# Output product in three f32r terms, with attention writing the high and low parts of its output

## Chip, cores and metric

One core of one Trainium2 chip. The metric is the device time of one execution in microseconds, from the start of the program to its end. The kernel before takes 3271.62 us (median of 3 runs).

## The reference

One decoder layer on 1024 tokens of width 1024, in float32, followed by a final RMSNorm:

```
h  = x + W_out [ DilatedWindowAttn(heads 0..7) || MLA(heads 8..15) ](RMSNorm(x) @ W_in)
h  = h + PEER(RMSNorm(h))
out = RMSNorm(h)
```

Heads 0 to 7 attend over three dilated windows whose results are merged (written in the kernel as one softmax with a mask of log counts); heads 8 to 15 are dense causal attention on low-rank projections. Each head gives 64 columns, so `mixed` is 1024 x 1024, and the part that the change is about is `h = x + mixed @ w_out`, with w_out 1024 x 1024. PEER then ranks product keys for each token (8 heads, 16 of 16384 experts each) and adds the gated outputs of the experts chosen.

## The kernel before, in words

The program runs stage after stage, with a barrier between: `project_in` (norm, input projection, rotary phases), `attend`, `project_out`, `route` (queries, keys, top 16, and the first expert activations), `spread_gates` and `run_experts`. Tokens are in 8 tiles of 128. Engines are programmed by hand, each with its own instruction list in program order, and meet at semaphores. TensorE is PE in the profile, VectorE DVE, ScalarE ACT, GpSimd POOL, SyncE SP.

`project_in` loads x as four pieces into `res`, which stays in SBUF until the end of `project_out`, where it serves as the residual.

`attend` (L521) works on 8 pairs of heads, four dilated and four dense. A pair p has 8 steps, one for each tile i of queries, and step s = 8p + i handles both heads against (i + 1) tiles of keys. There are 64 steps. Each engine's list is software-pipelined:

- TensorE, step s: `scores(s+1)` (L674), into banks 0 to 3; `turn(s)` (L685), transposes of the probabilities; `weigh(s-1)` (L700), the product with the values, into bank 6 or 7; and, where `due(s)` names any, `turn_head` (L654): transposes of the queries and keys of the next pair, into the same two banks.
- ScalarE, step s: copies of the turned probabilities of head 0 (L750), `exp(s+1)` of both heads (L741), `take(s-1)` (L747), which moves weigh's 128 x 128 result from PSUM to `mixT` in SBUF, and `copy_head` (L734) for the heads that are due.
- VectorE, step s: `masked(s+1, 0)` (L774), a copy of the turned probabilities of head 1 (L724), `masked(s+1, 1)`, further copies, and `normalise(s+1)` of both heads: a reciprocal (L782) and a scaling (L784).

The heads that are due are spread by two lists (L584), relative to the start of the pair before: one piece in each of steps 3, 4, 5, 6 for a dilated pair, pieces in steps 0, 0, 1, 2, 3, 4, 5, 6 for a dense one. What keeps the two output banks from being overwritten is the semaphore `o_out`, raised by `take`:

```
650                    need(pe, o_out, head_steps(p)[n] - 1)     # turn_head in step s: s - 1 counts
696                need(pe, o_out, s - 1)                        # weigh(s)
```

`scores(s)` waits for both `masked(s-1)`; `exp` waits for `masked` and for the `turn` that read the buffer last; `turn(s)` waits for `normalise(s)`.

`project_out` (L805) computes the product by tile: 16 f32 matmuls of 128x512 (L869) into two banks, `add` with the row of `res` (L931), the norm (L901, L905, L943), transposes of the normed row (L878), a copy of it (L948), and its split into `hn_hi` (L910, rounded to f32r) and `hn_lo` (L954, the rest). TensorE works a tile ahead: multiply(1) stands before the transposes of tile 0. SP loads g_ffn, the first w_pq columns and the first keys, and stores each tile's rows as the normed row gets ready.

`route` multiplies in three f32r terms already (L1116: hi x hi, lo x hi, hi x lo, each with 512 columns).

Of the kernel before, what the change touches and what calls it, by code (L numbers as in the profile page):

```python
# [6 lines left out]
P = 128  # L7
# [138 lines left out]
    return v.rearrange("(k p) -> p k", p=P)  # L146


def project_in(core, heads_a, heads_m, mask, mask_in):

    nc, ps, res = core.nc, core.ps, core.res
    I = core.i
    with ExitStack() as ctx:
        sb, sem = core.scope(ctx)
        w_in = sb("w_in", [P, KD, IN_W])
        w_uq = sb("w_uq", [P, 2, UQ_W])
        w_ukv = sb("w_ukv", [P, UKV_W])
        g_mix = sb("g_mix", [P, KD])
# [359 lines left out]
            pair(LAST, False)  # L518


def attend(core, mixT, mask, nat_a, nat_m, w_out, w_out_in):  # L521

    nc, ps = core.nc, core.ps
    PAIRS_A, PAIRS = HA // 2, (HA + HM) // 2
# [3 lines left out]
    with ExitStack() as ctx:  # L528
# [21 lines left out]
        rden_ready, normed, pv_done, o_out = sem("rden_ready"), sem("normed"), sem("pv_done"), sem("o_out")  # L550
# [176 lines left out]
        @block.scalar  # L727
        def _(act):
            def copy_head(p, n):
                k, z, half = pieces(p)[n]  # L730
                w = 2 * dim(p) if in_a(p) else dim(p)
                act.wait_ge(head_turned, pieces_before(p) + n + 1)
                need(act, score_done, 2 * NT * (p - 1))
                nc.scalar.activation(qk[0:w, slot(p, k, z), half * BANK:(half + 1) * BANK], ps[0:w, head_bank(p, n), :],  # L734
                                     ACT.Copy, scale=1.0 if z else -float(dim(p)) ** -0.5).then_inc(head_copied, 1)

            def exp(s, k):
                u, nk = 2 * s + k, (s % NT + 1) * P
                act.wait_ge(masked_ready, u + 1)
                need(act, turned[k], fills_before(s))  # L740
                nc.scalar.activation(pr[:, k, 0:nk], sm[:, k, 0:nk], ACT.Exp, scale=-1.0, bias=least[:, u:u + 1],  # L741
                                     accum_out=den[:, u:u + 1]).then_inc(prob_ready, 1)

            def take(s):
                p, i = s // NT, s % NT
                act.wait_ge(pv_done, s + 1)
                nc.scalar.activation(mixT[:, p, i * P:(i + 1) * P], ps[:, OUT_BANK + s % 2, 0:P], ACT.Copy  # L747
                                     ).then_inc(o_out, 1)

            copy = lambda out, src: nc.scalar.activation(out, src, ACT.Copy)  # L750
            for n in range(len(pieces(0))):
                copy_head(0, n)
            exp(0, 0)
            exp(0, 1)
            for s in range(STEPS):
                for f in range(len(fills(s))):
                    copy_fill(act, copy, s, 0, f)
                if s + 1 < STEPS:
                    exp(s + 1, 0)
                    exp(s + 1, 1)  # L760
                if s:
                    take(s - 1)
                for p, n in due(s):
                    copy_head(p, n)
            take(STEPS - 1)

        @block.vector
        def _(dve):
# [10 lines left out]
            def normalise(s, k):  # L779
# [4 lines left out]
                nc.vector.tensor_scalar(pr[:, k, 0:nk], pr[:, k, 0:nk], rden[:, u:u + 1], None, ALU.mult  # L784
                                        ).then_inc(normed, 1)

            copy = nc.vector.tensor_copy
            masked(0, 0)
            masked(0, 1)
# [14 lines left out]

def project_out(core, mix, w_out, w_out_in, hn_hi, hn_lo, w_raw, keys, pq_in):  # L805

    nc, ps, res = core.nc, core.ps, core.res
    with ExitStack() as ctx:
        sb, sem = core.scope(ctx)
        hn = sb("hn", [P, 2, D])  # L810
# [3 lines left out]
        h_sent = sem("h_sent")  # L814
        full = sb("hnT", [P, 2, KD, P])
        junk = sb("junk_o", [P, D], bf16)
        ss = sb("ss_o", [P, 2])
# [10 lines left out]
        def split_banks(k):  # L828

            return ps[:, 2 + 2 * k:4 + 2 * k, :]  # L830
# [5 lines left out]
            if not (isinstance(n, int) and n == 0):  # L836
                eng.wait_ge(sem_, ONE + n * 2 - 1 + k)

        def row(t, n, k):
            return t[:, n * 2 + k, :]  # L840

        def pairs(pair):
            for n in range(LAST + 1):
# [1 line left out]

        @block.sync
        def _(sp):
            sp.dma_start(g[:, :], core.i["g_ffn"].to_broadcast([P, D])).then_inc(g_in, 16)
            sp.dma_start(w_raw[:, :, :], core.i["w_pq"].rearrange("l (k p) n -> p (l k) n", p=P)[:, :, 0:PQ]
                         ).then_inc(pq_in, 16)  # L850
            sp.dma_start(keys[:, 0, :, :], core.i["sub_keys"].rearrange("l h z n c -> n (l h) z c")[:, 0, :, :]
                         ).then_inc(pq_in, 16)
            for i in range(NT):
                sp.wait_ge(hn_ready, ONE + i + 1)
                if i < GT:
                    sp.dma_start(core.scr_rows[:, i, :], hn[:, i % 2, :]).then_inc(row_sent[i % 2], 16)
                sp.dma_start(core.scr_h[:, i, :], res[:, i, :]).then_inc(h_sent, 16)
            for k in range(2):
                sp.wait_ge(row_sent[k], 16 * len(range(k, GT, 2)))
            sp.wait_ge(h_sent, 16 * NT)  # L860
            sp.wait_ge(pq_in, 32)

        @block.tensor
        def _(pe):
            def multiply(n, k):
                again(pe, h_ready, n, k)
                for c in range(2):
                    for j in range(KD):
                        last = nc.tensor.matmul(split_banks(k)[:, c, :],  # L869
                                                mix[:, j, (n * 2 + k) * P:(n * 2 + k + 1) * P],  # L870
                                                w_out[:, j, c * BANK:(c + 1) * BANK], start=j == 0, stop=j == KD - 1)
                last.then_inc(y_done, 1)

            def turn_hidden(n, k):
# [12 lines left out]
                multiply(n, 1)  # L887
                turn_hidden(n, 0)

            pe.wait_ge(w_out_in, 16)  # L890
            pairs(pair)
            turn_hidden(LAST, 1)

# [1 line left out]
        def _(act):  # L895
            own = Own(act, core.act_own)

            def norms(n, k):
                act.wait_ge(h_ready, ONE + n * 2 + k + 1)
                own.sync()  # L900
                own.mark(nc.scalar.activation(junk[:, :], row(res, n, k), ACT.Square, accum_out=ss[:, k:k + 1]))  # L901
# [11 lines left out]
            def pair(n, first, last):  # L913
# [4 lines left out]
                copy_hi(n, 0)  # L918
                own.restart()

            pairs(pair)
            copy_hi(LAST, 1)

        @block.vector
        def _(dve):
            own = Own(dve, core.dve_own)

            def add(n, k):
                dve.wait_ge(y_done, ONE + n * 2 + k + 1)
                h = row(res, n, k)  # L930
                nc.vector.tensor_tensor(h, split_banks(k).rearrange("p b n -> p (b n)"), h, ALU.add  # L931
                                        ).then_inc(h_ready, 1)

            def normalise(n, k):
# [8 lines left out]
                nc.vector.scalar_tensor_tensor(out=hn[:, k, :], in0=row(res, n, k), scalar=rstd[:, k:k + 1],  # L943
                                               in1=g[:, :], op0=ALU.mult, op1=ALU.mult).then_inc(hn_ready, 1)

            def copy_full(n, k):
# [10 lines left out]
            def pair(n, first, last):  # L957
# [1265 lines left out]
def layer(nc, ins, out):  # L2223
    with ExitStack() as ctx, ExitStack() as outer:
        core = Core(nc, ctx, ins, out)
        with ExitStack() as mid:
            sb, sem = core.scope(mid)
            core.res = sb("res", [P, NT, D])
# [7 lines left out]
            project_in(core, heads["a"], heads["m"], mask, mask_in)  # L2236
            mix = sb("mix_turned", [P, KD, SEQ])
            w_out = sb("w_out", [P, KD, D])
            attend(core, mix, mask, heads["a"], heads["m"], w_out, w_out_in)
            att.close()  # L2240
            hidden = outer.enter_context(ExitStack())
            hn_hi, hn_lo = (hidden.enter_context(nc.sbuf_tensor(n, [P, KD, SEQ], f32r, side="right"))
                            for n in ("hn_hi", "hn_lo"))
# [4 lines left out]
            project_out(core, mix, w_out, w_out_in, hn_hi, hn_lo, w_raw, keys, pq_in)  # L2248
# [63 lines left out]
```

## Time and profile before

| | us |
|---|---|
| median of 3 runs (3264.33 to 3278.61) | 3271.62 |
| the profiled execution | 3271.36 |
| its span | 3269.6 |
| of it `project_in` | 0 to 291 |
| `attend` | 291 to 614 |
| `project_out` | 614 to 742 |
| `route` and all behind it | 742 to 3269.6 |

Over the span TensorE is busy 91% of the time, VectorE 70%, ScalarE 30%, GpSimd 38%; the granted TensorE clock is 0.969 of 2.4 GHz on average. A share of busy time says only which engine a stage leans on; who waits for whom within a step is read from the instructions in order of time. In the rows of the profile, "out<-in" are the tiles written and read, and brackets at the end give the idle time before the instruction and what ended it.

### The profile page before, as it was taken

The numbers are of one execution on the slowest core, as the hardware profiler recorded it, in microseconds if no ns is written. First come the engines' busy times: TensorE is split into PE (matmuls) and PEld (weight loads), VectorE is DVE, ScalarE is ACT, GpSimd is POOL, SyncE is SP. The second block draws the span as 40 slices with busy tenths as digits, with TensorE's granted clock in tenths as the row PEclk, the third lists the DMA queues.
The fourth block names the chain that finished last, engine by engine and source line by source line (L and its number), as shares of the span: only waits on it lengthen the run. The fifth ranks groups of instructions, "written<-read, shape, count | busy, mean of one in ns | idle before, by whom it ended". The sixth has DMA issues, their size and how long they took to land.

```text
span 3269.6 us, 52312 instructions
## 1 busy us (share of the span) xinstructions
PE 2963.8 (91%) x19658; PEld 2423.8 (74%) x19658; DVE 2276.3 (70%) x5468; ACT 987.9 (30%) x1452; POOL 1258.3 (38%) x1088
## 2 busy tenths in 40 slices
PE   7997999997988666689999999999999999999997
PEld 4444666545777656689998888888888888888876
DVE  1213766436999789868977777777777887777435
ACT  2223665212222279722222221122222222222212
POOL 0000000001433400024457767676676776675241
PEclk9998999998999889999999999999999999999998
DMA  5213111112121127798899999999999999999694
GB/s 192 100 56 127 40 47 32 47 48 98 63 69 49 48 59 204 248 297 291 283 356 393 376 377 381 380 383 382 372 383 386 382 391 380 373 387 342 215 326 167
DMA packets 330175, 779.23 MB, mean 238 GB/s; under 512 B 45648, under 2 KB 147280, under 8 KB 328528
## 3 DMA queue, kind: packets, MB, share of 16 engines
q0 software_dynamic: 129024, 469.82, 38.1%
q1 hardware_dynamic: 178512, 288.92, 25.3%
q10 hardware_dynamic: 22400, 17.32, 1.6%
q8 instruction: 148, 2.42, 0.3%
q14 instruction: 91, 0.75, 0.1%
HBM read 699.42 MB, written 72.35 MB: 236 GB/s over the span
## 4 chain that ended last, share of the span: by engine, by line
PE 45%; DVE 11%; DMA 5%; issue 2%; POOL 1%; ACT 0%; SPq 0%; DVEq 0%; ACTq 0%
PE psum L1882 20%; PE psum L1866 19%; PE psum L1908 5%; DVE first L1551 4%; DMA u_ring<-u_rows,eid 3%; DVE one L1544 1%; DMA scr_g<-gates 1%; DVE acc L2071 1%; DVE u_ring L2079 1%; POOL v_ring L1839 1%; DVE u_lo L2035 1%; DVE second L1554 1%; DVE v_lo L2057 1%; DMA v_ring<-v_rows,eidT 1%; DMA v_raw<-v_rows 0%
## 5 line engine op out<-in xcount | busy, mean ns | idle before, releaser
L1839 POOL DMA_INDIRECT v_ring<-v_rows,eidT x448 | 596.1, 1331 | 410.2 <-PE psum L1908 300.6
L1831 POOL DMA_INDIRECT u_ring<-u_rows,eid x448 | 510.8, 1140 | 283.4 <-DVE dots L2079 178.4
L2079 DVE CUSTOM_DVE_ANT_0 u_ring<-u_ring,rows 128x1024 f32<-128x1024 f32 x448 | 544.8, 1218 | 106.6 <-DMA u_ring<-u_rows,eid 105.4
L1866 PE MATMUL psum<-hn_hi_e,u_hi 128*128 128x288 f32 x1792 | 530.1, 296 | 8.4 <-SPq L108 5.0
L1866 PE MATMUL psum<-hn_lo_e,u_hi 128*128 128x288 f32 x1792 | 528.0, 295 | 0.0
L1866 PE MATMUL psum<-hn_hi_e,u_lo 128*128 128x288 f32 x1792 | 527.7, 294 | 0.0
L1882 PE MATMUL psum<-w_hi,v_hi 128*128 128x288 f32 x2048 | 464.0, 309 | 55.1 <-DVE acc L2071 39.9
L2071 DVE TENSOR_TENSOR acc<-psum,acc 128x576 f32<-128x576 f32 x504 | 379.9, 754 | 144.5 <-PE psum L1882 135.8
L1882 PEld LDWEIGHTS psum<-w_hi,v_hi 128*128 128x128 f32 x2048 | 336.6, 194 | 152.8 <-issue 99.3
L1882 PE MATMUL psum<-w_hi,v_lo 128*128 128x288 f32 x2048 | 448.5, 301 | 0.0
L1882 PE MATMUL psum<-w_lo,v_hi 128*128 128x288 f32 x2048 | 448.2, 301 | 0.0
L1866 PEld LDWEIGHTS psum<-hn_hi_e,u_hi 128*128 128x128 f32 x1792 | 337.5, 188 | 14.0 <-issue 14.0
L1882 PEld LDWEIGHTS psum<-w_hi,v_lo 128*128 128x128 f32 x2048 | 339.8, 194 | 0.0
L1882 PEld LDWEIGHTS psum<-w_lo,v_hi 128*128 128x128 f32 x2048 | 339.5, 194 | 0.0
L1866 PEld LDWEIGHTS psum<-hn_lo_e,u_hi 128*128 128x128 f32 x1792 | 336.9, 188 | 0.0
L1866 PEld LDWEIGHTS psum<-hn_hi_e,u_lo 128*128 128x128 f32 x1792 | 336.8, 188 | 0.0
L1969 ACT ACTIVATE psum<-psum 128x576 f32<-128x576 f32 x112 | 71.1, 635 | 854.6 <-PE psum L1866 854.6
L1980 ACT ACTIVATE v_hi<-v_raw 128x1024 fp32r<-128x1024 f32 x128 | 128.8, 1053 | 394.8 <-PE psum L1882 383.0
L2047 DVE TENSOR_TENSOR w<-psum,w 128x576 f32<-128x576 f32 x112 | 84.8, 757 | 206.6 <-ACT psum L1969 206.3
L1908 PE MATMUL psum<-v_ring,strip 128*32 128x512 f32 x1792 | 218.7, 606 | 8.3 <-DMA v_ring<-v_rows,eidT 8.3
L1569 PE MATMUL psum<-second,first 128*128 128x128 f32 x1152 | 147.8, 282 | 72.8 <-DVE second L1554 72.6
L473 PE MATMUL psum<-w_in,hT 128*128 128x512 f32 (+1 forms) x512 | 211.5, 575 | 0.0
(236 smaller groups left out, 4208.4 us busy)
## 6 DMA issues: line engine op xcount, KB each, us to landing
v_raw<-v_rows SPq DMA_DIRECT2D x128, 512.0 KB, 7.2
u_raw<-uT SPq DMA_DIRECT2D x112, 512.0 KB, 8.0
w<-scr_g SPq DMA_DIRECT2D x128, 288.0 KB, 5.9
scr_g<-gates SPq DMA_DIRECT2D x3, 8192.0 KB, 30.6
scr_m<-st_m SPq DMA_DIRECT2D x8, 1024.0 KB, 4.0
w_raw<-in_w_pq SPq DMA_DIRECT2D x8, 1024.0 KB, 7.0
u_raw_r<-uT SPq DMA_DIRECT2D x16, 512.0 KB, 3.6
scr_g<-gates ACTq DMA_DIRECT2D x1, 7680.0 KB, 36.5
```

Of the source, the lines that this page charges most:

```text
L473: last = nc.tensor.matmul(ps[:, 2 + c, 0:width(c)], hT[:, k, j, :], w_in[:, j, c * BANK:c * BANK + width(c)], start=j == 0, stop=j == KD - 1)
L1551: nc.vector.tensor_scalar(first[:, b, t, :], iota_f[:, :], flat[:, 0, at:at + 1], flat[:, 2, at:at + 1], ALU.is_equal, ALU.mult).then_inc( ...
L1569: last = nc.tensor.matmul(slot, first[:, b, t, :], second[:, b, t, :], start=True, stop=True)
L1831: pool.indirect_dma_start(u_ring[:, n % U_RING, :], None, core.i["u_rows"], bass.IndirectOffsetOnAxis(eid[:, x // 2, x % 2, k:k + 1], 0)). ...
L1839: pool.indirect_dma_start(v_ring[:, m % V_RING, :], None, core.i["v_rows"], bass.IndirectOffsetOnAxis(eidT[:, x // 2, col:col + 1], 0)).th ...
L1866: last = nc.tensor.matmul(ps[:, a, 0:COLS], x[:, c, j, :], y[:, j, a * COLS:(a + 1) * COLS], start=m == 0, stop=m == len(terms) - 1)
L1882: last = nc.tensor.matmul(ps[:, OUT_AT + F % OUT_PAIRS * 2 + a, 0:COLS], x[:, c, f * P:(f + 1) * P], y[:, b, c, a * COLS:(a + 1) * COLS], ...
L1908: last = nc.tensor.matmul(ps[k * WIDE:(k + 1) * WIDE, SUM_AT + half, :], strip[:, p % 2, at:at + WIDE], v_ring[:, n % V_RING, half * BANK: ...
L1980: nc.scalar.activation(v_hi[:, c, :], v_raw[:, c, :], ACT.Copy).then_inc(v_hi_ready, 1)
L2047: nc.vector.tensor_tensor(half, ps[:, 0:ACTS, 0:COLS], half, ALU.mult).then_inc(w_ready, 1)
L2071: nc.vector.tensor_tensor(into, ps[:, at:at + 2, 0:COLS], into, ALU.add).then_inc(added, 1)
L2079: nc.vector.tensor_tensor_reduce(out=u, in0=u, in1=rows[:, x % 2, :], scale=1.0, scalar=0.0, op0=ALU.mult, op1=ALU.add, accum_out=dots[:, ...
```

## The change

1. Attention's output is written in two parts, into the places where `hn_hi` and `hn_lo` of the normed rows will lie: `take` on ScalarE writes the f32r-rounded value and raises `hi_out`; a new `low` on VectorE subtracts that from the PSUM value, writes the f32r rest and raises `o_out`. On VectorE `low(s-2)` is the last operation of step s.
2. The output product is 48 f32r matmuls a tile instead of 16 f32 ones. `w_out` is split first, by eight slices: ScalarE rounds into `w_hi`, VectorE subtracts into `w_lo`, which lies where `w_out` lay.
3. `res` is freed after `project_in`; `project_out` loads x again, a tile at a time, into three row buffers from which the rows are also stored.
4. `w_in` moves to the other end of SBUF, with rows of 2048 elements instead of 1952, so that `hn_hi` and `hn_lo` take its place after it.

```diff
@@ attend @@
@@ scalar: take @@
-                nc.scalar.activation(mixT[:, p, i * P:(i + 1) * P], ps[:, OUT_BANK + s % 2, 0:P], ACT.Copy
-                                     ).then_inc(o_out, 1)
+                nc.scalar.activation(mix_hi[:, p, i * P:(i + 1) * P], ps[:, OUT_BANK + s % 2, 0:P], ACT.Copy
+                                     ).then_inc(hi_out, 1)
@@ vector @@
+            def low(s):
+                p, i = s // NT, s % NT
+                dve.wait_ge(hi_out, s + 1)
+                nc.vector.tensor_tensor(mix_lo[:, p, i * P:(i + 1) * P], ps[:, OUT_BANK + s % 2, 0:P],
+                                        mix_hi[:, p, i * P:(i + 1) * P].bitcast(f32), ALU.subtract).then_inc(o_out, 1)
...
                 if s + 1 < STEPS:
                     normalise(s + 1, 0)
                     normalise(s + 1, 1)
+                if s > 1:
+                    low(s - 2)
+            low(STEPS - 2)
+            low(STEPS - 1)
@@ project_out, sync @@
+            x_v = core.i["x"].rearrange("b (i p) d -> p (b i) d", p=P)
+            def load_x(i):
+                sp.dma_start(h[:, i % XB, :], x_v[:, i, :]).then_inc(x_in[i % XB], 16)
+            for i in range(XB):
+                load_x(i)
             sp.dma_start(g[:, :], core.i["g_ffn"].to_broadcast([P, D])).then_inc(g_in, 16)
...
             for i in range(NT):
                 sp.wait_ge(hn_ready, ONE + i + 1)
+                sp.dma_start(core.scr_h[:, i, :], h[:, i % XB, :]).then_inc(h_sent[i % XB], 16)
                 if i < GT:
                     sp.dma_start(core.scr_rows[:, i, :], hn[:, i % 2, :]).then_inc(row_sent[i % 2], 16)
-                sp.dma_start(core.scr_h[:, i, :], res[:, i, :]).then_inc(h_sent, 16)
+                if i + XB < NT:
+                    sp.wait_ge(h_sent[i % XB], 16 * (i // XB + 1))
+                    load_x(i + XB)
@@ tensor: multiply @@
-                for c in range(2):
-                    for j in range(KD):
-                        last = nc.tensor.matmul(split_banks(k)[:, c, :],
-                                                mix[:, j, (n * 2 + k) * P:(n * 2 + k + 1) * P],
-                                                w_out[:, j, c * BANK:(c + 1) * BANK], start=j == 0, stop=j == KD - 1)
+                for j in range(KD):
+                    if n == 0 and k == 0:
+                        pe.wait_ge(w_lo_ready, j + 1)
+                    for t, (x, y) in enumerate(((hn_hi, w_hi), (hn_lo, w_hi), (hn_hi, w_lo))):
+                        for c in range(2):
+                            last = nc.tensor.matmul(split_banks(k)[:, c, :], x[:, j, tokens],
+                                                    y[:, j, c * BANK:(c + 1) * BANK],
+                                                    start=j == 0 and t == 0, stop=j == KD - 1 and t == 2)
@@ scalar, ahead of the tiles @@
+            act.wait_ge(w_out_in, 16)
+            for j in range(KD):
+                nc.scalar.activation(w_hi[:, j, :], w_out[:, j, :], ACT.Copy).then_inc(w_hi_ready, 1)
@@ vector: add, and ahead of the tiles @@
+                dve.wait_ge(x_in[i % XB], 16 * (i // XB + 1))
...
+            for j in range(KD):
+                dve.wait_ge(w_hi_ready, j + 1)
+                nc.vector.tensor_tensor(w_lo[:, j, :], w_out[:, j, :], w_hi[:, j, :].bitcast(f32), ALU.subtract
+                                        ).then_inc(w_lo_ready, 1)
```

`attend` gets `hn_hi` and `hn_lo` for `mixT`; `turn_head` and `weigh` keep their waits for `o_out` word for word.

## Rows read from the trace of the kernel before

**Rows 1.** Busy time by stretch: attention (first two) and the output product.

```profile
core 0: us, PE busy (x) PEld busy (x) DVE busy (x) ACT busy (x) POOL busy (x), PEclk, DMA share, GB/s
291.00:408.00 117.00, 105.77 (x856) 69.49 (x858) 86.40 (x243) 71.60 (x181) 3.51 (x1) 0.93 0.24 78
408.00:614.40 206.40, 188.32 (x1452) 127.17 (x1448) 138.32 (x366) 114.84 (x286) 3.51 (x1) 1.00 0.11 32
614.40:742.00 127.60, 117.95 (x321) 55.80 (x322) 41.14 (x49) 20.01 (x34) 0.00 (x0) 0.97 0.16 63
```

**Rows 2.** Order of time, one dense pair: start us, duration us, engine, line.

```profile
445.50 0.35 DVE L784 TENSOR_SCALAR pr<-pr,rden 128x256 f32<-128x256 f32 x1
...
445.80 0.64 PE L654 MATMUL psum<-ident,qn_m 128*96 128x128 f32 x4
...
449.86 0.64 PE L654 MATMUL psum<-ident,qn_m 128*96 128x128 f32 x4
...
451.46 0.42 DVE L784 TENSOR_SCALAR pr<-pr,rden 128x384 f32<-128x384 f32 x1
...
458.54 0.64 PE L654 MATMUL psum<-ident,qn_m 128*96 128x128 f32 x4
...
460.46 0.55 DVE L784 TENSOR_SCALAR pr<-pr,rden 128x640 f32<-128x640 f32 x1
...
461.78 0.96 DVE L774 CUSTOM_DVE_ANT_0 sm<-psum,mask 128x768 f32<-128x768 f32 x1 [0.77 <-PE psum L674]
...
464.75 0.92 ACT L741 ACTIVATE pr<-sm,least 128x768 f32<-128x768 f32 x1
...
465.12 0.64 PE L654 MATMUL psum<-ident,kn_m 128*96 128x128 f32 x4
...
466.00 0.62 DVE L784 TENSOR_SCALAR pr<-pr,rden 128x768 f32<-128x768 f32 x1
...
479.71 0.64 PE L654 MATMUL psum<-ident,kn_m 128*96 128x128 f32 x4
...
480.80 0.76 DVE L784 TENSOR_SCALAR pr<-pr,rden 128x1024 f32<-128x1024 f32 x1
```

**Rows 3.** Groups of the product's stage, by line.

```profile
L954 DVE TENSOR_TENSOR hn_lo<-hnT,hn_hi 128x1024 fp32r<-128x1024 f32 x8 | 9.8, 1219 | 1.2 <-ACT hn_hi L910 1.2
...
L910 ACT ACTIVATE hn_hi<-hnT 128x1024 fp32r<-128x1024 f32 x8 | 8.3, 1043 | 3.7 <-DVE hnT L948 3.7
```

**Rows 4.** Order of time, the first masked operation of attention.

```profile
295.18 0.29 DVE L774 CUSTOM_DVE_ANT_0 sm<-psum,mask 128x128 f32<-128x128 f32 x1 [11.07 <-PE psum L674]
```

**Rows 5.** Order of time on TensorE, behind idle stretches.

```profile
614.47 27.70 PE L869 MATMUL psum<-w_out,mix_turned 128*128 128x512 f32 x64 [1.78 <-PEq L99]
...
778.94 3.61 PE L1116 MATMUL psum<-hn_hi,w_hi 128*128 128x512 f32 x8 [1.88 <-issue]
...
910.48 2.13 PE L1116 MATMUL psum<-hn_hi,w_hi 128*128 128x512 f32 x8 [3.37 <-DVE w_lo L1409]
...
956.08 3.35 PE L1116 MATMUL psum<-hn_hi,w_hi 128*128 128x512 f32 x8 [3.49 <-DVE w_lo L1409]
...
1093.21 2.29 PE L1096 MATMUL psum<-hn_hi,u_hi_r 128*128 128x288 f32 x8 [2.25 <-ACT u_hi_r L1170]
```

**Rows 6.** Busy time near the start of attention.

```profile
303.00:309.00 6.00, 5.65 (x22) 2.96 (x24) 3.78 (x14) 3.04 (x9) 0.00 (x0) 0.50 1.03 409
```

**Rows 7.** Order of time on TensorE: the same scores in pairs 0 and 1.

```profile
299.37 1.65 PE L674 MATMUL psum<-qk_turned 64*128 64x384 f32 x4 [0.76 <-DVE least L774]
...
313.52 1.56 PE L674 MATMUL psum<-qk_turned 64*128 64x512 f32 x8
...
338.78 0.92 PE L674 MATMUL psum<-qk_turned 64*128 64x384 f32 x4
...
348.45 1.56 PE L674 MATMUL psum<-qk_turned 64*128 64x512 f32 x8
```

**Rows 8.** Order of time on TensorE, f32r matmuls of the routing stage.

```profile
768.32 2.03 PE L1116 MATMUL psum<-hn_hi,w_hi 128*128 128x512 f32 x8
770.19 2.03 PE L1116 MATMUL psum<-hn_lo,w_hi 128*128 128x512 f32 x8
```

**Rows 9.** DMA issue of w_out: KB each, median us from issue to landing.

```profile
w_out<-in_w_out SPq DMA_DIRECT2D x1, 4096.0 KB, 16.0
```

More of the change, by code:

```diff
@@ L146, in column, with project_in @@
     return v.rearrange("(k p) -> p k", p=P)
-def project_in(core, heads_a, heads_m, mask, mask_in):
+def project_in(core, w_in, heads_a, heads_m, mask, mask_in):
     nc, ps, res = core.nc, core.ps, core.res
@@ L154, in project_in @@
         sb, sem = core.scope(ctx)
-        w_in = sb("w_in", [P, KD, IN_W])
         w_uq = sb("w_uq", [P, 2, UQ_W])
@@ L518, in _, with attend @@
             pair(LAST, False)
-def attend(core, mixT, mask, nat_a, nat_m, w_out, w_out_in):
+def attend(core, mix_hi, mix_lo, mask, nat_a, nat_m, w_out, w_out_in):
     nc, ps = core.nc, core.ps
@@ L549, in attend @@
         copied = [sem(f"copied{k}") for k in range(2)]
-        rden_ready, normed, pv_done, o_out = sem("rden_ready"), sem("normed"), sem("pv_done"), sem("o_out")
+        rden_ready, normed, pv_done = sem("rden_ready"), sem("normed"), sem("pv_done")
+        hi_out, o_out = sem("hi_out"), sem("o_out")
         zero_low, zero_high = sem("zero_low"), sem("zero_high")
@@ L802, in _, with project_out @@
                     normalise(s + 1, 1)
-def project_out(core, mix, w_out, w_out_in, hn_hi, hn_lo, w_raw, keys, pq_in):
-    nc, ps, res = core.nc, core.ps, core.res
+                if s > 1:
+                    low(s - 2)
+            low(STEPS - 2)
+            low(STEPS - 1)
+def project_out(core, w_out, w_lo, w_out_in, hn_hi, hn_lo, w_raw, keys, pq_in):
+    nc, ps = core.nc, core.ps
+    XB = 3
     with ExitStack() as ctx:
         sb, sem = core.scope(ctx)
+        w_hi = sb("w_out_hi", [P, KD, D], f32r)
+        h = sb("h", [P, XB, D])
         hn = sb("hn", [P, 2, D])
@@ L813, in project_out @@
         row_sent = [sem(f"row_sent{k}") for k in range(2)]
-        h_sent = sem("h_sent")
+        x_in = [sem(f"x_in_o{k}") for k in range(XB)]
+        h_sent = [sem(f"h_sent{k}") for k in range(XB)]
+        w_hi_ready, w_lo_ready = sem("w_hi_ready_o"), sem("w_lo_ready_o")
         full = sb("hnT", [P, 2, KD, P])
@@ L837, in again, with row @@
                 eng.wait_ge(sem_, ONE + n * 2 - 1 + k)
-        def row(t, n, k):
-            return t[:, n * 2 + k, :]
+        def row(n, k):
+            return h[:, (n * 2 + k) % XB, :]
         def pairs(pair):
@@ L854, in _ @@
                 sp.wait_ge(hn_ready, ONE + i + 1)
+                sp.dma_start(core.scr_h[:, i, :], h[:, i % XB, :]).then_inc(h_sent[i % XB], 16)
                 if i < GT:
                     sp.dma_start(core.scr_rows[:, i, :], hn[:, i % 2, :]).then_inc(row_sent[i % 2], 16)
-                sp.dma_start(core.scr_h[:, i, :], res[:, i, :]).then_inc(h_sent, 16)
+                if i + XB < NT:
+                    sp.wait_ge(h_sent[i % XB], 16 * (i // XB + 1))
+                    load_x(i + XB)
             for k in range(2):
                 sp.wait_ge(row_sent[k], 16 * len(range(k, GT, 2)))
-            sp.wait_ge(h_sent, 16 * NT)
+            for k in range(XB):
+                sp.wait_ge(h_sent[k], 16 * len(range(k, NT, XB)))
             sp.wait_ge(pq_in, 32)
@@ L866, in multiply @@
                 again(pe, h_ready, n, k)
-                for c in range(2):
-                    for j in range(KD):
-                        last = nc.tensor.matmul(split_banks(k)[:, c, :],
-                                                mix[:, j, (n * 2 + k) * P:(n * 2 + k + 1) * P],
-                                                w_out[:, j, c * BANK:(c + 1) * BANK], start=j == 0, stop=j == KD - 1)
+                tokens = slice((n * 2 + k) * P, (n * 2 + k + 1) * P)
+                for j in range(KD):
[6 more added lines that the diff above has]
+                                                    start=j == 0 and t == 0, stop=j == KD - 1 and t == 2)
                 last.then_inc(y_done, 1)
@@ L900, in norms @@
                 own.sync()
-                own.mark(nc.scalar.activation(junk[:, :], row(res, n, k), ACT.Square, accum_out=ss[:, k:k + 1]))
+                own.mark(nc.scalar.activation(junk[:, :], row(n, k), ACT.Square, accum_out=ss[:, k:k + 1]))
                 own.sync()
@@ L929, in add @@
                 dve.wait_ge(y_done, ONE + n * 2 + k + 1)
-                h = row(res, n, k)
-                nc.vector.tensor_tensor(h, split_banks(k).rearrange("p b n -> p (b n)"), h, ALU.add
+                i = n * 2 + k
+                dve.wait_ge(x_in[i % XB], 16 * (i // XB + 1))
+                nc.vector.tensor_tensor(row(n, k), split_banks(k).rearrange("p b n -> p (b n)"), row(n, k), ALU.add
                                         ).then_inc(h_ready, 1)
@@ L942, in normalise @@
                     dve.wait_ge(row_sent[k], 16 * n)
-                nc.vector.scalar_tensor_tensor(out=hn[:, k, :], in0=row(res, n, k), scalar=rstd[:, k:k + 1],
+                nc.vector.scalar_tensor_tensor(out=hn[:, k, :], in0=row(n, k), scalar=rstd[:, k:k + 1],
                                                in1=g[:, :], op0=ALU.mult, op1=ALU.mult).then_inc(hn_ready, 1)
@@ L2225, in layer @@
         core = Core(nc, ctx, ins, out)
+        hidden = outer.enter_context(ExitStack())
+        with nc.sbuf_tensor("hn_hi", [P, KD, SEQ], f32r, side="right") as hn_hi, \
+                nc.sbuf_tensor("hn_lo", [P, KD, SEQ], f32r, side="right") as hn_lo:
+            pass
+        w_in = hidden.enter_context(nc.sbuf_tensor("w_in", [P, KD, 2 * SEQ], f32, side="right"))
         with ExitStack() as mid:
-            sb, sem = core.scope(mid)
-            core.res = sb("res", [P, NT, D])
+            _, sem = core.scope(mid)
             att = ExitStack()
@@ L2235, in layer @@
             clear_counts(nc, (mask_in, w_out_in))
[L2236 to L2239, printed above, removed]
+            with ExitStack() as front:
+                core.res = front.enter_context(nc.sbuf_tensor("res", [P, NT, D], f32))
+                project_in(core, w_in, heads["a"], heads["m"], mask, mask_in)
+            with nc.sbuf_tensor("w_out_lo", [P, KD, D], f32r) as w_lo:
+                pass
+            w_out = mid.enter_context(nc.sbuf_tensor("w_out", [P, KD, D], f32))
+            attend(core, hn_hi, hn_lo, mask, heads["a"], heads["m"], w_out, w_out_in)
             att.close()
-            hidden = outer.enter_context(ExitStack())
-            hn_hi, hn_lo = (hidden.enter_context(nc.sbuf_tensor(n, [P, KD, SEQ], f32r, side="right"))
-                            for n in ("hn_hi", "hn_lo"))
             w_raw = hidden.enter_context(nc.sbuf_tensor("w_raw", [P, KD, PQ], f32, side="right"))
@@ L2247, in layer @@
             clear_counts(nc, (pq_in,))
-            project_out(core, mix, w_out, w_out_in, hn_hi, hn_lo, w_raw, keys, pq_in)
+            project_out(core, w_out, w_lo, w_out_in, hn_hi, hn_lo, w_raw, keys, pq_in)
         with ExitStack() as peer:
```

1 line of the change is left out of this document (removed).

## The prediction

> **What bounds the kernel now.** I read the busy time by stage first. Attention runs from 291 to 614 us, the output product from 614 to 742; TensorE is busy 90, 91 and 92% of the three stretches, at a granted clock of 0.93, 1.00 and 0.97 [rows 1]. So TensorE bounds both stages that the diff touches, and two kinds of edit can move the time: TensorE work taken away, and TensorE made to wait. VectorE has room on average (86.40 + 138.32 us busy in 323) [rows 1], but what counts is when it is done within a step, and for that I read the order of time.
>
> In a step s of attention TensorE issues scores(s+1), turn(s), weigh(s-1) and, in 40 of the 64 steps, turn_head, the transposes that prepare the next pair of heads. Two lists in the code give the 40: steps 3 to 6 of the first three pairs, and steps 0 to 6 of pairs 3 to 6 (two pieces in their step 0): 12 + 28. ScalarE and VectorE meanwhile do exp(s+1) and normalise(s+1), each of two heads. The trace shows TensorE starting turn_head BEFORE the second normalise(s+1) has ended: at 465.12 against 466.62, right behind weigh(s-1), while the second exponential had begun only at 464.75 [rows 2]. Today this is free, since turn_head waits only for the take of step s-2, done by ScalarE a step earlier.
>
> **The change in attention.** ScalarE's take stays, now writing the high part; rounding costs it nothing (a 1024-wide copy into f32r takes 1043 ns, with 128x1024 f32 in) [rows 3]. New is low(s-2) on VectorE, 64 in all, a 128x128 operation with one operand in PSUM; the nearest row of that shape, engine and source is 0.29 us [rows 4]. 64 x 0.29 = 19 us in a stage where VectorE idles some 98 us: as work it is covered. But o_out is now raised by low, and low(s-2) stands in VectorE's order BEHIND both normalise(s+1). turn_head in step s waits for s-1 counts of o_out, that is for low(s-2). So TensorE now waits in each of the 40 steps until VectorE has finished the next step's normalisation, and only then issues turn_head and, behind it, scores(s+2). Before, scores(s+2) covered exactly that latency.
>
> The price of one wait is: end of the second normalise, plus 0.29 for low, minus the start of turn_head today. From the pairs of [rows 2]:
> step 0 of a pair: 445.50+0.35+0.29-445.80 = 0.34;
> step 1: 451.46+0.42+0.29-449.86 = 2.31;
> step 3: 460.46+0.55+0.29-458.54 = 2.76;
> step 4: 466.00+0.62+0.29-465.12 = 1.79;
> step 6: 480.80+0.76+0.29-479.71 = 2.14.
> Steps 2 and 5 read the same way give 2.55 and 1.98. The pattern repeats in all four long blocks (13.9 each) and, as steps 3 to 6, in three short ones (8.6 each): 4 x 13.9 + 3 x 8.6 = 81.4 us. A release from VectorE to TensorE adds about 0.05 each: 2 us.
>
> Does the delay stay, or is it made up? exp(s+2) follows turn(s+1), and masked(s+2) follows scores(s+2): at 461.78 VectorE had been idle 0.77 us for them [rows 2]. Both follow turn_head on TensorE, so a late turn_head moves the whole loop. What is given back are TensorE's present waits for VectorE in these steps, 3 to 4 us by my count. Where no head is due (24 steps) low sits ahead of the next masked and costs at most 0.29 in the few that VectorE bounds: 2 to 3 us; the last low adds 0.35 to the end. These cancel. Attention: **+82 us**, between 70 (more absorbed) and 85. weigh(s-1) waits for low(s-3) too, which follows the normalise that turn(s) needs anyway: nothing. ScalarE's copy_head and SP's loads for the next heads stand behind turn_head and come later with it; they have a step and more of room.
>
> **The clock.** Each wait is a stretch of idle TensorE, 1.8 to 2.8 us long in steps 1 to 6. What the trace shows of such stretches is mixed [rows 5]: after 1.88 us idle eight 512-column matmuls took 3.61 us, after 3.49 us 3.35, but after 3.37 us 2.13; after 2.25 us eight of 288 columns took 2.29. The stretch from 303 to 309 has a granted clock of 0.50 (1.2 GHz) [rows 6]. Of nine idle stretches from 1.5 to 1.8 us, in the routing stage and before the product, none was followed by slow matmuls; of six from 1.8 to 3.9 us five were (the longest of the nine, 1.78, and four of the six have their rows [rows 5]). What the low clock costs: the same steps took 313.52-299.37 = 14.15 us in pair 0, nearly all of it at half clock, and 348.45-338.78 = 9.67 in pair 1 [rows 7]: 4.5 lost in 14.1, 0.32 us per us. If half of the 36 long waits let the clock fall, for 6 us each (about 3 in the routing stage, 12 at the start of attention, where TensorE was busy 5.65 of 6 us and still slow [rows 6]), that is 18 x 6 x 0.32 = **+35 us**. The bounds are 0 and 36 x 8 (about one lengthened step) x 0.32 = 92.
>
> **The change in the product.** Two tiles of 16 f32 matmuls each take 27.70 us, 13.8 a tile [rows 5] (two records per matmul). In their place come 48 f32r matmuls of the same 128x512 shape. The routing stage runs just that: eight from 768.32 to 770.19, 0.234 us each [rows 8], so 48 are 11.2 us. Saved: 2.55 x 8 = 20.4 us, if TensorE stays the bound, and it does: VectorE has five operations near 1.22 us in a tile of 12 and ScalarE less.
> Against it, ahead of the first tile: ScalarE makes w_hi in 8 copies of 1.04, VectorE w_lo in 8 of 1.22 [rows 3]. The first matmul starts after one of each, 2.3 us, and then TensorE's six matmuls per slice (1.4) are slower than VectorE's next slice (1.22), so the rest is hidden. The idle stretch before the product thus grows from 1.78 [rows 5] to about 4.4 us, longer than any that kept the clock; some 4.6 us at half speed do 2.3 us of work, another 2.3 us lost. Sum: -20.4 + 2.3 + 2.3 = **-15.8 us**.
> The residual rows now come by tile: three loads of 512 KB stand on SP's queue ahead of g_ffn, w_raw and keys. By 4096 KB in 16.0 us [rows 9] the first 2 MB land in about 8 us, and the first addition is due after 2.3 + 11.2. Later rows start after the store of the tile three before, 512 KB each way, about 2 us each by the same row, and have two tiles of time: nothing, or at worst one late tile, 5 us. w_raw and keys are needed 110 us later. w_in's rows are wider in SBUF and elsewhere; the same bytes and matmuls: nothing.
>
> **Sum.** The profiled run took 3271.36 us for a span of 3269.6, 0.3 below the median of 3271.62. 3271.4 + 82 + 35 - 16 = **3372 us**.
>
> **The rivals.**
> (a) The wait comes, but the clock holds, in attention and at the product's start: 3271.4 + 82 - 18 = 3336. For it: the clock in 408 to 614 is 1.00 with small gaps everywhere [rows 1]. Against it: five of the six stretches above [rows 5]. 0.22.
> (b) The half clock stays through nearly all of the steps concerned, since TensorE did not leave it for 12 us at the start [rows 6, 7]: 3271.4 + 82 + 92 - 16 = 3429. 0.12. The Trainium skill, TensorE: Matmul & The Clock Gate, section "HAM oscillation — how this bites in real kernels", says that a kernel whose bursts of matmuls alternate with waits can have its clock throttled anew at every burst. By this rule it would come out as (b); the trace agrees in five stretches of the six and not in the one of 3.37 us.
> (c) The other side: the wait is hidden. It decides by one order, low(s-2) against weigh(s-1): if VectorE reached low before TensorE ends weigh, only the product's gain is left, 3271.4 - 16 + 2 = 3257. Weigh would have to last 2 to 3 us longer, or the exponentials start earlier, and they wait for turn(s). 0.05, mostly within 0.5% (16 us, about what a measurement of this kernel can tell from no change).
> (d) The product does not run at the routing stage's rate (the w slices or the row loads pace it), so that the gain is nil, and attention is as forecast: 3388. 0.06.
> Forecast: 0.55.
>
> **Numbers.** The range goes from 3325 (rival a with 10 us more absorbed) to 3425 (short of b); beyond it lie most of b, and c. Faster 0.02, same 0.04, slower 0.94.
>
> **What would show it.** In the trace of after: TensorE's transposes of natural heads (the qn and kn tiles) idle some 80 us in all, released by VectorE's subtraction into the low part, none of it before; their idle is 1.8 to 2.8 each, 0.3 in step 0; attention lasts 400 to 445 us instead of 323, with a granted clock below 1.00 in many stretches; tiles of the product begin 12.1 us apart instead of 14.6. It is wrong if those transposes start right behind weigh, if the clock column stays at 9 in attention while the span grows by more than 90, or if the product's stage is not shorter by 10 to 20 us.

## The result, and the profile after

The changed kernel takes 3359.88 us (median of 4 runs, 3350.44 to 3364.98) against 3270.23 for the kernel before (4 runs, one more than ahead of the prediction): a ratio of 1.0269, 95% interval 1.0236 to 1.0302, 90 us slower. The forecast was 3372, within 3325 to 3425. The profiled execution took 3357.79 us, for a span of 3356.0, 86.4 more than the span before.

The page of the kernel after, its slices of TensorE's busy time and of its granted clock, 84 us each:

```profile
PE   8997776788888856679999999999999999999997
PEclk9997889998999979999999999999999999999998
```

Attention lies in slices 4 to 9. TensorE is down to 6 to 8 tenths there, and the granted clock is at 7, 8 and 8 in slices 4 to 6. By stretches (us, busy time, granted clock, share and rate of the DMA), TensorE in attention from its first instruction to its last:

```profile
core 0: us, PE busy (x), PEclk, DMA share, GB/s
293.75:361.00 67.25, 53.44 (x364) 0.81 0.34 110
361.00:455.00 94.00, 70.76 (x530) 0.87 0.07 18
455.00:506.00 51.00, 39.05 (x273) 0.80 0.11 32
506.00:708.60 202.60, 151.49 (x1142) 1.00 0.09 24
```

Where [rows 1] had 90 and 91% busy, it is now 79, 75, 77 and 75%, and the clock of 0.81 to 0.87 lasts until 506 us. Then it is 1.00, while the busy share stays as low. Who waited for whom in the same stage (us in total, times, the longest):

```profile
PE psum L654 <- issue: 64.9, 33, 2.7
PE psum L654 <- DVE hn_lo L790: 13.0, 7, 2.7
PE psum L654 <- ACT qk_turned L734: 3.1, 4, 0.8
```

TensorE is idle 64.9 + 13.0 = 77.9 us before the transposes of the next heads, 40 times, at most 2.7. Seven of them the trace ascribes to the new subtraction (`low`, L790), 33 to nothing that it shows ("issue"); before the change there was only the third row. That the 33 too are waits for `low` shows in the order of time: in all 40 the transposes start 0.06 or 0.10 us after the end of a `low`. Step 1 of a pair, on VectorE and TensorE:

```profile
511.57 0.42 DVE L784 TENSOR_SCALAR pr<-pr,rden 128x384 f32<-128x384 f32 x1
511.91 0.28 DVE L790 TENSOR_TENSOR hn_lo<-psum,hn_hi 128x128 fp32r<-128x128 f32 x1
```

The second scaling ends at 511.99, `low` at 512.19, and the transposes start at 512.29. One pair of heads in order of time, to be laid beside [rows 2]:

```profile
505.93 0.61 PE L654 MATMUL psum<-ident,qn_m 128*96 128x128 f32 x4 [0.29 <-issue]
...
512.29 0.61 PE L654 MATMUL psum<-ident,qn_m 128*96 128x128 f32 x4 [2.26 <-issue]
...
518.35 0.61 PE L654 MATMUL psum<-ident,kn_m 128*96 128x128 f32 x4 [2.48 <-issue]
...
525.51 0.61 PE L654 MATMUL psum<-ident,qn_m 128*96 128x128 f32 x4 [2.70 <-issue]
...
533.45 0.61 PE L654 MATMUL psum<-ident,kn_m 128*96 128x128 f32 x4 [1.74 <-issue]
...
542.40 0.61 PE L654 MATMUL psum<-ident,qn_m 128*96 128x128 f32 x4 [1.99 <-issue]
...
552.19 0.61 PE L654 MATMUL psum<-ident,kn_m 128*96 128x128 f32 x4 [2.07 <-issue]
...
560.71 0.61 PE L654 MATMUL psum<-ident,qn_m 128*96 128x128 f32 x4 [0.29 <-issue]
```

Each long step has its idle time in brackets: 2.26, 2.48, 2.70, 1.74, 1.99, 2.07, and 0.29 in step 0. From one step 0 to the next it is 560.71 - 505.93 = 54.78 us, at full clock; before, 42.69 (from 445.80 to the next step 0):

```profile
488.49 0.64 PE L654 MATMUL psum<-ident,qn_m 128*96 128x128 f32 x4
```

The last `take` of attention and the product, after:

```profile
708.61 0.28 ACT L747 ACTIVATE hn_hi<-psum 128x128 fp32r<-128x128 f32 x1 [1.47 <-PE psum L700]
...
713.03 1.22 PE L899 MATMUL psum<-w_out_hi,hn_hi 128*128 128x512 f32 x2 [4.47 <-DVE w_out_lo L1005]
...
714.90 1.05 PE L899 MATMUL psum<-w_out_lo,hn_hi 128*128 128x512 f32 x2
...
715.76 1.05 PE L899 MATMUL psum<-w_out_hi,hn_hi 128*128 128x512 f32 x2
...
721.48 0.63 PE L899 MATMUL psum<-w_out_hi,hn_hi 128*128 128x512 f32 x2
...
721.95 0.63 PE L899 MATMUL psum<-w_out_hi,hn_lo 128*128 128x512 f32 x2
...
738.34 1.03 PE L908 MATMUL psum<-ident,hn 128*128 128x128 f32 x8
...
750.46 1.03 PE L908 MATMUL psum<-ident,hn 128*128 128x128 f32 x8
...
823.90 0.69 PE L1141 MATMUL psum<-ident,keys 128*128 128x128 f32 x2 [6.21 <-SPq L1101]
```

The product starts after 4.47 us of idle time instead of 1.78 [rows 5] and at half clock: a pair of matmuls starts 0.86 us behind the one before it at 715.76, and 0.47 at 721.95, which is 0.234 us a matmul. The tiles' transposes come 750.46 - 738.34 = 12.12 us apart instead of 14.61. From the last take to the first transposes of the routing stage (L1141) it is 115.3 us against 129.2 before.

The 86.4 us of the span: `project_in` +2.5 (293.75 against 291.26 for attention's first transposes), attention +93.4 (414.9 against 321.5, first transposes to last take), product -13.9, everything behind it +4.4. The first and the last are not the change's: in the other kernels below, attention starts anywhere from 290.4 to 293.7 us, whether `w_in` lies at the one end or the other, and the stages after the product last 2523 to 2530 us, against 2528 before the change and 2532 here.

### The profile page after: what moved, and what is told of

It reads as the page before. It is cut to its first block, busy times and chain, and to the rows that moved or that the text cites. A ratio compares the mean times of both kernels' runs of the same rounds, so it can differ in the third digit from the quotient of the medians.

```text
span 3356.0 us, 52665 instructions
## 1 busy us (share of the span) xinstructions
PE 2968.6 (88%) x19786; PEld 2461.5 (73%) x19786; DVE 2300.2 (69%) x5540; ACT 999.6 (30%) x1460; POOL 1263.8 (38%) x1088
## 4 chain that ended last, share of the span: by engine, by line
PE 43%; DVE 11%; DMA 5%; issue 3%; POOL 1%; ACT 0%; SPq 0%; DVEq 0%; ACTq 0%
PE psum L1919 19%; PE psum L1903 19%; PE psum L1945 5%; DVE first L1588 4%; DMA u_ring<-u_rows,eid 3%; DVE one L1581 1%; DVE acc L2108 1%; DMA scr_g<-gates 1%; DVE u_ring L2116 1%; POOL v_ring L1876 1%; DVE u_lo L2072 1%; DVE v_lo L2094 1%; DVE second L1591 1%; DMA v_ring<-v_rows,eidT 1%; DMA v_raw<-v_rows 0%
```

## The experiments

Each was timed beside the kernel before on the same chip. Attention's length is taken as above.

**e1_low_early.** The theory is one of order, so the first run changes the order alone:

```diff
-                if s > 1:
-                    low(s - 2)
-            low(STEPS - 2)
+                if s:
+                    low(s - 1)
             low(STEPS - 1)
```

> After, with low(s-1) instead of low(s-2) at the end of VectorE's step s, so that o_out stands a step earlier for turn_head. Theory (turn_head's wait behind the next normalise is the whole loss): the 78 us of idle time before the transposes L654 are gone, the clock in attention is 1.00 from about 312 us on as in before, and only the product's gain of some 10 to 16 us is left: 3250 to 3262. Rival (64 more operations on VectorE, or the f32r parts, cost the time): it stays above 3330. Rival (the wait goes to another place: low(s-1) now waits for take(s-1), and VectorE with it): idle time of VectorE before low of 0.3 us or more in each of 64 steps, and 3270 to 3290.

3254.66 us (3250.24 to 3256.27), ratio 0.9952 (0.9937 to 0.9967): faster than before by 14 us and than the changed kernel by 105. Waits, and the line of `low` in attention:

```profile
PE psum L654 <- ACT qk_turned L734: 3.1, 4, 0.8
L790 DVE TENSOR_TENSOR hn_lo<-psum,hn_hi 128x128 fp32r<-128x128 f32 x63 | 18.0, 285 | 7.5 <-ACT hn_hi L747 7.5
```

The idle time before the transposes is gone but for the 3.1 us that were there before; 64 subtractions are still made. `low` now waits for ScalarE's take, 7.5 us in all where the rival wanted 19, and nobody pays: attention is 320.4 us long, 1 less than before. So neither the work nor the new layout costs anything; the place in VectorE's order does.

**e2_low_between.** A middle dose:

```diff
                 if s + 1 < STEPS:
                     normalise(s + 1, 0)
-                    normalise(s + 1, 1)
                 if s > 1:
                     low(s - 2)
+                if s + 1 < STEPS:
+                    normalise(s + 1, 1)
```

> After, with low(s-2) between the two normalise(s+1) instead of behind both. Theory: each long wait gets shorter by the time from the end of the first to the end of the second scaling (0.9 to 1.1 us by the trace), times 36, so 32 to 40 us less idle before L654, and fewer falls of the clock: 3300 to 3325. Rival (the number of operations or the clock alone counts, not where low stands): within 5 us of after, 3355 to 3365.

3286.45 us (3284.05 to 3294.03), ratio 1.0056 (1.0035 to 1.0077): 14 us below the expected band. The waits, and TensorE in attention from 312 us on:

```profile
PE psum L654 <- issue: 34.1, 30, 1.6
PE psum L654 <- DVE hn_lo L790: 6.8, 6, 1.6
```

```profile
312.00:648.50 336.50, 275.38 (x2240) 1.00 0.11 32
```

The idle time fell by 37 us, to 40.9, as expected, and the longest is 1.6 us. What was not expected: the clock never fell after 312 us. Attention is 354.8 us, 33.4 more than before, so 40.9 us of waits cost 33.4: 7.5 us are made up elsewhere.

**e3_wait_alone.** The kernel before, with nothing but the wait:

```diff
                     need(pe, o_out, head_steps(p)[n] - 1)
+                    pe.wait_ge(normed, 2 * (head_steps(p)[n] + 2))
```

> Before, with one wait more: turn_head waits until both normalise(s+1) are done. No low, no f32r product, res kept. Theory: 36 waits of 1.5 to 2.5 us and 4 of 0.05, 82 - 40 x 0.29 = 70 us, and the clock's share of 15 to 30: 3355 to 3370. Rival (the loss comes from low as work, or from the new layout of SBUF): under 3300.

3359.06 us (3357.86 to 3371.64), ratio 1.0286 (1.0262 to 1.0309): attention's loss with no f32r part at all, 90.4 of the 93.4 us (411.9 against 321.5). That the time is the changed kernel's own is chance: that one has the product's 13.9 us taken off and 6.9 us added outside both stages. Its waits, and two of its transposes:

```profile
PE psum L655 <- DVE pr L785: 63.7, 32, 2.7
PE psum L655 <- ACT mix_turned L748: 11.9, 6, 2.5
```

```profile
517.81 0.78 PE L655 MATMUL psum<-ident,kn_m 128*96 128x128 f32 x4 [1.70 <-DVE pr L785]
...
528.41 1.06 PE L655 MATMUL psum<-ident,qn_m 128*96 128x128 f32 x4 [1.94 <-DVE pr L785]
```

75.6 us idle, 70 expected. At 528.41, after 1.94 us of idle time, four transposes take 1.06 us instead of 0.61: the wait alone brings the clock down as well, here also after 506 us (the mean over the rest of attention):

```profile
506.00:702.30 196.30, 151.50 (x1085) 0.95 0.08 22
```

The expectation took the whole 0.29 us of `low` off each wait, 11.6 in all; the idle time is only 2.3 us under the changed kernel's 77.9. The order of time shows why. Step 1 of a pair here:

```profile
611.77 0.42 DVE L785 TENSOR_SCALAR pr<-pr,rden 128x384 f32<-128x384 f32 x1
612.45 0.61 PE L655 MATMUL psum<-ident,qn_m 128*96 128x128 f32 x4 [2.21 <-DVE pr L785]
```

From the end of the second scaling to the transposes it is 612.45 - 612.19 = 0.26 us, and 512.29 - 511.99 = 0.30 in the changed kernel; over the 40 waits the means are 0.23 and 0.29. So the release by the scaling alone takes nearly as long as `low` with its own release, and 40 x 0.06 = 2.4 us are the difference.

**e4_work_alone.** The kernel before, with the work and no wait:

```diff
+        spare = sb("spare", [P, P], f32r)
...
+            def low(s):
+                p, i = s // NT, s % NT
+                dve.wait_ge(o_out, s + 1)
+                at = mixT[:, p, i * P:(i + 1) * P]
+                nc.vector.tensor_tensor(spare[:, :], at, at, ALU.subtract)
...
                     normalise(s + 1, 1)
+                if s > 1:
+                    low(s - 2)
```

> Before, with 64 subtractions of 128x128 on VectorE at the place of low(s-2), reading mixT and writing a scrap tile, for which nobody waits. Theory: hidden in VectorE's idle time, 0 to 4 us: 3270 to 3274. Rival (VectorE is the bound of attention's steps): +19 us or more, 3289 and above.

3271.57 us (10 runs, 3267.33 to 3279.25), ratio 1.0008 (0.9998 to 1.0018). 62 operations of 284 ns in VectorE's list, for steps 0 to 61, are hidden: attention is 320.4 us long, 1 less than before. They read SBUF, where those of the changed kernel read PSUM, and last as long.

**e5_kept_warm.** The changed kernel, with the wait kept and its idle time filled:

```diff
+                if p and head_steps(p)[n] % NT:
+                    pe.wait_ge(masked_ready, 2 * (head_steps(p)[n] + 2))
+                    for _ in range(FILL):
+                        nc.tensor.matmul(ps[:, 0, 0:P], v_of(p - 1)[:, 0, :], v_of(p - 1)[:, 0, :],
+                                         start=True, stop=True)
                 if p:
                     need(pe, o_out, head_steps(p)[n] - 1)
```

`FILL` is 7. The idle matmuls write bank 0 and so wait for the masks that read it (`masked_ready`).

> After, with seven matmuls of 128x128 f32 (1.5 us in all, by the transposes' rate) that nobody reads, into bank 0, ahead of turn_head's wait in the 36 long steps. The wait itself stays: turn_head starts no earlier. Theory (the clock took about 23 us of attention's 93): granted clock 1.00 in attention from about 312 us on, TensorE's idle before L654 down to some 25 to 30 us, and 3335 to 3345. Rival (the clock costs nothing, since the path runs over the other engines): within 5 us of after, 3355 to 3365. Rival (matmuls in the way delay turn_head): above 3370.

3324.68 us (3322.98 to 3326.04), ratio 1.0168 (1.0153 to 1.0183): 35 us less than the changed kernel for more work, more than the theory gave (26 and 23 less than the two later executions of the changed kernel, below). Order of time on TensorE in one step, the wait that is left, and the stage by stretches:

```profile
461.14 1.83 PE L653 MATMUL psum<-v_more 128*128 128x128 f32 x14
...
463.08 0.64 PE L660 MATMUL psum<-ident,qn_m 128*96 128x128 f32 x4
...
471.48 0.64 PE L660 MATMUL psum<-ident,kn_m 128*96 128x128 f32 x4 [0.16 <-DVE hn_lo L796]
```

```profile
core 0: us, PE busy (x), PEclk, DMA share, GB/s
290.80:312.00 21.20, 17.09 (x90) 0.69 0.79 273
312.00:682.60 370.60, 336.15 (x2720) 1.00 0.09 27
```

The fourteen records at 461.14 are the seven idle matmuls; behind them the transposes wait 0.3 us at most. They still start 0.06 to 0.10 us after the end of `low`, in four of the 40 steps 0.13 to 0.19, so the wait itself is kept. The clock is 1.00 from 312 us to the end. Attention is 391.9 us: 23.0 less than in the changed kernel at the same waits, and 70.4 more than before. That splits attention's 93.4 us: 70.4 for the waits, 23.0 for the clock. The other 12 of the 35 us lie outside attention (3 before it, and the stages behind it, where the two kernels are the same): not explained, and of the size by which those stages differ between executions.

**e6_f32_product.** e1_low_early, with the product as one f32 term of the high part, and no split of w_out:

```diff
...
-                    for t, (x, y) in enumerate(((hn_hi, w_hi), (hn_lo, w_hi), (hn_hi, w_lo))):
-                        for c in range(2):
-                            last = nc.tensor.matmul(split_banks(k)[:, c, :], x[:, j, tokens],
-                                                    y[:, j, c * BANK:(c + 1) * BANK],
-                                                    start=j == 0 and t == 0, stop=j == KD - 1 and t == 2)
+                for c in range(2):
+                    for j in range(KD):
+                        last = nc.tensor.matmul(split_banks(k)[:, c, :], hn_hi[:, j, tokens].bitcast(f32),
+                                                w_out[:, j, c * BANK:(c + 1) * BANK], start=j == 0, stop=j == KD - 1)
...
```

> e1_low_early with the product in one f32 term, 16 matmuls a tile of the high part with w_out, without the split of w_out; left out of the computation: the low part of attention's output. Attention, loads and stores as in e1. Theory: tiles 14.6 us apart instead of 12.1 and a start without the 4.5 us idle: +20 - 5 = +15 against e1's 3254.7, so 3266 to 3273, level with before. Rival (e1's gain comes from attention or from the row loads, not from the product): within 4 us of e1.

3269.77 us (12 runs, 3262.28 to 3276.63), ratio 0.9996 (0.9986 to 1.0007): 15.1 more than e1 by the medians, 14 by the ratios (the two ran on different chips), and level with before. So e1's gain is the three-term product's. In this kernel the stretch from the last take to the routing stage's transposes is 740.84 - 611.57 = 129.3 us, the 129.2 of before, though its residual rows come by tile: the new loads are hidden.

**e7_first_slice.** e1_low_early, with the first slice of w_out split in attention's last two steps (`w_first`, 4 KB a partition):

```diff
@@ attend, scalar, ahead of step 62's copies @@
+                    nc.scalar.activation(w_first[:, j, :], w_out[:, j, :], ACT.Copy).then_inc(first_hi, 1)
@@ attend, vector, behind step 63's copies @@
+                nc.vector.tensor_tensor(w_lo[:, j, :], w_out[:, j, :], w_first[:, j, :].bitcast(f32), ALU.subtract
+                                        ).then_inc(first_lo, 1)
@@ project_out @@
-            for j in range(KD):
+            for j in range(AHEAD, KD):
```

> e1_low_early with the first of the eight slices of w_out split in attention's last two steps, where ScalarE and VectorE wait for TensorE. Theory: the product starts some 1.8 us after attention instead of 4.5, the clock holds there (saves 2.3 to 2.8), then one wait of up to 1 us for the second slice: 4 to 5 us less than e1, 3249 to 3252. Rival (the split delays attention's last steps by as much): no difference from e1.

3252.92 us (3246.31 to 3253.87), ratio 0.9942 (0.9930 to 0.9955) against e1's 0.9952: the intervals overlap, so no difference can be told. The product's start:

```profile
613.80 0.71 PE L917 MATMUL psum<-w_first,hn_hi 128*128 128x512 f32 x2 [2.12 <-PEq L99]
...
616.15 1.22 PE L917 MATMUL psum<-w_out_hi,hn_hi 128*128 128x512 f32 x2 [0.65 <-DVE w_out_lo L1023]
```

The product starts after 2.12 us of idle time, and the first six matmuls run at full speed. Then TensorE waits 0.65 for the second slice, and the matmuls behind it take twice the time: the fall of the clock was not avoided, only moved. The 0.65 us are not its cause, since the clock is down from about 615.2 us on and that wait begins at 615.50. Nor do the 2.12 us decide it by their length: in e6_f32_product the product starts after the same idle time and the clock holds. The clock by stretches in e7:

```profile
613.00:615.20 2.20, 1.40 (x6) 1.00 0.29 37
615.20:619.00 3.80, 3.15 (x9) 0.51 0.95 371
```

The first matmuls and the clock in e6:

```profile
613.64 2.81 PE L895 MATMUL psum<-w_out,hn_hi 128*128 128x512 f32 x6 [2.12 <-PEq L99]
...
613.00:617.00 4.00, 3.36 (x8) 1.00 0.57 176
```

From the last take to the routing stage it is 113.9 us against 115.0 in e1.

**e8_after_again, e9_after_third.** Two more executions of the changed kernel, with their profiles:

> The changed kernel once more, unchanged, for a second profile. In the first one the clock fell in attention only up to about 505 us, though the same waits of 1.7 to 2.7 us went on to 660. If the falls depend on where a wait happens to lie, and not on the step of the program, this profile has them in other stretches, and attention (415 us in the first) is 400 to 430 us long, with idle time before L654 again at 76 to 80 us. Rival (the steps of the second half cannot bring the clock down): it is again 1.00 from 505 us on and attention within 2 us of 415.

> As e8_after_again: a third profile, with the half clock in stretches of its own, or, by the rival, in the same ones as in the first.

3350.39 and 3347.30 us, one run each. TensorE in the second profile, from 361 us on:

```profile
361.00:455.00 94.00, 73.11 (x528) 0.84 0.07 18
455.00:506.00 51.00, 38.76 (x274) 0.80 0.12 33
506.00:707.20 201.20, 150.82 (x1138) 1.00 0.08 24
```

Attention is 415.8 and 414.4 us long, with 78.1 us idle before the transposes in both; the clock is 0.84, 0.80 and 1.00 in these stretches in both. The falls end at the same place, about 500 us, in three executions of three, though the stretches before differ somewhat (0.87 against 0.84 between 361 and 455 us), so chance from one execution to the next does not spread them. Nor is it that the later steps could not bring the clock down: in e3_wait_alone it is 0.95 from 506 us to the end of attention, at waits of the same length. What decides it is open.

## Why the prediction was right

The mechanism came as forecast, and both of its terms were too large: the wait's by 11.6 us and the clock's by 12.0. That the sum is no further off is in part luck, as 6.9 us outside both stages went the other way.

**The wait.** The order in the code was read rightly: `low(s-2)` behind both `normalise(s+1)` holds up `turn_head`, and e1, which moves one line, takes all of it away; e3 brings it back by itself. Its size, step by step, was forecast as 0.34, 2.31, 2.55, 2.76, 1.79, 1.98 and 2.14, and measured 0.29, 2.26, 2.48, 2.70, 1.74, 1.99 and 2.07; 81.4 + 2 in sum against 77.9. The release from VectorE to TensorE that the forecast added at 0.05 is there, 0.06 or 0.10 us. What it left out is that `low` starts 0.08 us before the end of the scaling (511.91 against 511.99), so that from that end to the transposes it is 0.29 us and not 0.29 + 0.05; and that the idle time is counted from the end of the matmuls before, which is later than the start of `turn_head` in the trace of before (449.93 against 449.86 in step 1).

**Whether the delay stays.** Forecast: given back and added cancel, +82 in all, with 70 as the lower bound. Measured: +70.4 (e5). 77.9 us of waits cost 7.5 less than their sum, the same 7.5 as in e2 with half the waits. 3.4 of it are the older waits of `turn` and `scores` (L685 and L674) for VectorE and ScalarE, which sum to 18.2 us after the change and to 21.6 before, where 3 to 4 had been forecast; the rest was not followed. The step that erred is the one by which "these cancel": the 2 to 3 us for the steps without heads do not show (attention is 320.4 us long in e4 and in e1, 321.5 before).

**The clock.** Forecast +35, as 108 us at half clock at 0.32 each; measured +23.0 (e5 against the changed kernel). The extent was half of that: by the stretches of the profile after, 67.25 x 0.19 x 2 + 94 x 0.13 x 2 + 51 x 0.20 x 2 = 70 us stand at half clock, against 13 (21.2 x 0.31 x 2) in e5, so 57 more. The price was higher: 23.0 / 57 = 0.40 us per us. The two errors went against each other, which is luck: that half of the long waits would bring the clock down was a guess. Rival (a), in which the clock holds, is what e5 is as far as attention goes, at 3325 instead of 3336 (its terms add up to 3335). Rival (b) did not come: of the 18 long waits after 506 us not one brought the clock down in three executions, while in e3 such waits did. The prediction read (b) out of the Trainium skill, TensorE: Matmul & The Clock Gate, "HAM oscillation — how this bites in real kernels", by which bursts of matmuls between waits are throttled anew each time; but the waits in that section's example are longer than the 2.7 us that the longest lasts here, so it did not speak for (b), and no run here tests it.

**The product.** Forecast -15.8: -20.4 for the rate, +2.3 for the split ahead, +2.3 for the clock. Measured -13.9 in the changed kernel, -14.2 in e1 (115.0 against 129.2), and 14 to 15 between e6 and e1. The tile period is the forecast one, 12.1 us. The first matmul came after 4.47 us of idle time (4.4 forecast), and some 14 matmuls at 0.427 instead of 0.234 us cost 14 x 0.19 = 2.7 us (2.3 forecast). The rate gave 14.61 - 12.12 = 2.49 us a tile, 19.9 in all; the forecast's own 13.8 - 11.2 would be 2.6 and not the 2.55 that it took. With 4.47 - 1.78 = 2.7 us more idle time at the start these make -14.5; the other 0.6 were not followed. Rival (d), a product without a gain, is out by e6.

**Nothing for the residual rows**: e6 shows it, 129.3 against 129.2.

**The sum** was +101 and the span grew by 86.4, 14.6 less: 11.6 and 12.0 too much for the waits and the clock, 1.9 too much for the product's gain, and 6.9 us in `project_in` and the stages behind that the forecast did not have (-11.6 - 12.0 + 1.9 + 6.9 = -14.8, the rest is rounding). By the medians it was 12 us too high.

Rival (c), the hidden wait, is what e1 brings about by its order: 3254.7 against its 3257.

## What to carry to other kernels

When a semaphore gets a new raiser, ask not what the new operation costs but where it stands in its engine's list, and who, on the engine that bounds, waits for that place: 18 us of hidden work cost 93, and one line of reordering gave it all back. The price of such a wait can be read off the trace before the change is built, as the end of what the new raiser stands behind minus the start of what waits for it. Idle time of a bounding TensorE can have a second price in its clock, here a third on top of the first (23.0 on 70.4 us), and in e2, with waits of at most 1.6 us, none.

## What was not expected of the hardware

- Waits of at most 1.6 us (e2, 40.9 us in all) left the clock at 1.00, waits of 1.7 to 2.7 us brought it down in some stretches and not in others; in three executions of the changed kernel the last fall was at about 500 us, and in e3, with waits as long, there were later ones. What decides it is not shown.
- Seven matmuls that nobody reads, put into an idle time of about 2 us, made attention 23.0 us shorter (e5). The other 12 of the 35 us between the two kernels are not shown to be theirs.
- After an idle stretch of the same 2.12 us at the start of the product the clock held in e6 and fell in e7, there with six matmuls at full speed in between.
